# ScalarE's order in the input segments of the mixers: the split of a coming weight panel ahead of the correction copy

## What is computed

```python
def first_block(x, ...):
    for i in range(4):
        h = h + 0.5 * rmsnorm(swiglu(rmsnorm(h, gn[0]), ffn1_w_in[i], ffn1_w_out[i]), gn[1])
        hn = rmsnorm(h, gn[2])
        m = hgrn2_mixer(hn, ...)         # i = 0, 3; diff_attention: i = 1; pool_mixer: i = 2
        h = h + rmsnorm(m, gn[3])
        h = h + 0.5 * rmsnorm(swiglu(rmsnorm(h, gn[4]), ffn2_w_in[i], ffn2_w_out[i]), gn[5])

def second_block(x, ...):                # layer 0: hybrid_mixer, layer 1: recurrent_mixer
    ...

def hgrn2_mixer(x, w_in, gnorm_w, w_out, lb):
    q, f_pre, i_in, g = jnp.split(x @ w_in, ...)         # 1024 x 4096: the input projection
    f = lb + (1.0 - lb) * jax.nn.sigmoid(f_pre); k = 1.0 - f; log_f = jnp.log(f)
    ...                                                  # decayed scores in blocks, state, norm, gate
    return o @ w_out
```

## Time and profile before

| | us |
|---|---|
| median of 3 runs (3299.59 to 3308.34) | 3305.91 |
| the profiled execution, its own time | 3306.95 |
| its span, first to last instruction | 3305.2 |
| TensorE busy (PE) | 3144.2 |
| VectorE busy (DVE) | 2266.2 |
| ScalarE busy (ACT) | 1716.3 |
| mean granted clock of TensorE, share of full speed | 0.975 |
| HBM read, MB | 530.99 |

### The profile page before, as it was taken

The page is one execution under the profiler, slowest core; times in us unless marked ns, Lnnn a source line. Parts: engine busy times, 40 slices in busy tenths (PEclk is TensorE's granted clock), DMA queues, the critical chain, the costliest instruction groups (busy, mean ns, idle before and its releaser), DMA issues.

```text
span 3305.2 us, 44853 instructions
## 1 busy us (share of the span) xinstructions
PE 3144.2 (95%) x18084; PEld 2734.1 (83%) x18084; DVE 2266.2 (69%) x2748; ACT 1716.3 (52%) x2078; POOL 4.3 (0%) x21
## 2 busy tenths in 40 slices
PE   9998999998899999999998899999896999999998
PEld 8886888887688888888887788888774888888887
DVE  7667585867476775675857667585874585866674
ACT  6455554645355554554645555554442464655553
POOL 0000000000000000000000000000000000000000
PEclk9998999999899999999999999999996999999999
DMA  6542355454245454454553245455340255454353
GB/s 228 187 163 102 117 190 191 179 191 140 89 166 191 178 188 171 151 191 166 202 186 134 98 145 191 175 190 184 139 153 13 103 193 191 177 191 163 144 190 128
DMA packets 75358, 534.80 MB, mean 162 GB/s; under 512 B 8480, under 2 KB 8608, under 8 KB 10784
## 3 DMA queue, kind: packets, MB, share of 16 engines
q1 hardware_dynamic: 75168, 532.07, 44.7%
HBM read 530.99 MB, written 1.05 MB: 161 GB/s over the span
## 4 chain that ended last, share of the span: by engine, by line
PE 82%; DVE 8%; ACT 5%; DVEq 3%; issue 1%; DMA 0%; SPq 0%; ACTq 0%
PE pp L1905 33%; PE pp L1906 17%; PE pm L1905 8%; PE pp L2029 4%; PE pm L1906 4%; PE pp L1928 4%; DVE wlo L1675 2%; PE pp L1900 2%; PE pp L1899 2%; PE pp L1901 2%; PE pp L1930 2%; ACT whi L1513 2%; ACT corr L1580 1%; DVE mix L1842 1%; DVEq L395 0%
## 5 line engine op out<-in xcount | busy, mean ns | idle before, releaser
L1905 PE MATMUL pp<-xs,whi 128*128 128x512 f32 x4848 | 1710.1, 397 | 17.5 <-DVE tsum L1755 15.8
L1675 DVE TENSOR_TENSOR wlo<-raw,whi 128x2048 fp32r<-128x2048 f32 x477 | 1090.6, 2289 | 423.8 <-ACT whi L1513 423.0
L1906 PE MATMUL pp<-xs,wlo 128*128 128x256 f32 x4848 | 1357.7, 280 | 0.0
L1905 PEld LDWEIGHTS pp<-xs,whi 128*128 128x128 f32 x4848 | 915.6, 189 | 236.8 <-issue 28.1
L1513 ACT ACTIVATE whi<-raw 128x2048 fp32r<-128x2048 f32 x477 | 910.1, 1911 | 285.7 <-DMA raw<-weights 284.7
L1906 PEld LDWEIGHTS pp<-xs,wlo 128*128 128x128 f32 x4848 | 920.9, 190 | 0.7 <-issue 0.2
L1580 ACT ACTIVATE corr<-pp 128x512 f32<-128x512 f32 x352 | 209.2, 594 | 566.3 <-PE pp L1906 540.9
L1755 DVE TENSOR_TENSOR tsum<-pp,corr 128x512 f32<-128x512 f32 x339 | 233.6, 689 | 297.9 <-ACT corr L1580 297.1
L1905 PE MATMUL pm<-hs,whi 128*128 128x512 f32 x1120 | 393.8, 392 | 0.0
L1906 PE MATMUL pm<-hs,wlo 128*128 128x256 f32 x1120 | 313.2, 280 | 0.0
L1905 PEld LDWEIGHTS pm<-hs,whi 128*128 128x128 f32 x1120 | 210.3, 188 | 43.4
(11 more groups left out here) (330 smaller groups left out, 2989.4 us busy)
## 6 DMA issues: line engine op xcount, KB each, us to landing
raw<-weights SPq DMA_DIRECT2D x503, 1024.0 KB, 4.8
raw<-weights SPq DMA_DIRECT2D x8, 256.0 KB, 7.5
h<-x_by_feature SPq DMA_DIRECT2D x4, 256.0 KB, 6.5
out<-h SPq DMA_DIRECT2D x4, 256.0 KB, 2.5
vec<-vectors SPq DMA_DIRECT2D x1, 264.0 KB, 2.7
lamrow<-diff_lambda SPq DMA_DIRECT2D x1, 128.0 KB, 10.8
skiprow<-ssm_d SPq DMA_DIRECT2D x1, 8.0 KB, 12.5
```

The lines of the kernel that those rows point to most:

```text
L1675: v.tensor_tensor(wlo[:, slot, :], raw[:, slot, :], whi[:, slot, :].bitcast(F32), ALU.subtract).then_inc(sem("weights_lo"), 1)
L1905: mm(bank, whi[:, slot, c:c + P], x_k, start=start, stop=False)
L1906: return mm(bank[:, 0:T], wlo[:, slot, c:c + P], x_k[:, 0:T], start=False, stop=stop)
```

## The change

In `read_out` of ScalarE the split of panel p+4 is made before the wait for the product of panel p, in input segments: in the first one of a mixer from p = 3 on, in HYB's second one for every p. Closing segments keep the old order.

```diff
                 for p in range(seg.wide, seg.panels - closing):
+                    early = not closing and (after_first is None or p >= 3)
+                    if early:
+                        split(seg.g0 + p + AHEAD)
                     act.wait_ge(sem("panel_done"), seg.g0 + p + 1)
                     if seg.wide:
                         act.wait_ge(sem("panel_out"), seg.r0 + p - seg.wide - 1)
                     copy_corr(banks_of(seg, p), (p + seg.first_half) % 2)
                     if after_first is not None and p <= 2:
                         split(seg.g0 + p + AHEAD - 1)
-                    if after_first is None or p >= 2:
+                    if not early and (after_first is None or p >= 2):
                         split(seg.g0 + p + AHEAD)
                     if closing:
                         square_output(s, p - seg.wide)
```

## The result

| | us |
|---|---|
| changed kernel, median of 4 runs (3334.21 to 3341.05) | 3335.51 |
| kernel before, median of 4 runs (3299.59 to 3308.34) | 3305.20 |
| ratio, with its 95% interval | 1.0097 (1.0079 to 1.0115) |
| profiled execution after, its own time (before 3306.95) | 3334.33 |
| its span, with a mean granted clock of 0.972 (before 3305.2, 0.975) | 3332.6 |

The change makes the kernel slower by about 1%. The forecast of 3334 lies 1.5 us from the median. Read by stages it is less exact than that. In the profile after, lines of the kernel behind the edit stand three higher (L1755 is L1758, L1675 is L1678, L1842 is L1845, L1905 is L1908).

The account below looks back on a forecast made before the run. The prediction took the ScalarE-VectorE turn in HGRN, not TensorE, as the bound. HGRN 25.0, DIFF 2.4 and HYB 1.0 sum to 28.4 us on 3306.95, 3335.3; with the median 1.0 lower, 3334 us, range 3326 to 3343.

Parts of the forecast that it names:

- The bound in HGRN: HGRN stages: ScalarE's time between the last step of panel p-1 and what releases VectorE is on the path, once a panel.
- 1.39 a turn, nine times in each stage, 12.5: HGRN: each of nine moved panels a stage takes 1.39 us longer, about 12.5 us a stage, 25.0 us in both.
- 1.80: HGRN, each panel: time lost at the copy because the split holds ScalarE first; also the upper bound for a panel.
- 0.41: Each moved panel: us won at VectorE's wlo, which no longer waits for the split whi.
- What follows the last copy of the stage moves as a block: End of each HGRN stage: everything behind the last copy shifts together, with no further loss.
- The rival of the clock: Three stages: longer TensorE waits bring more lower-clock stretches, up to 16 us, half taken: 8, giving 3342; chance 0.08.
- DIFF +2.4: DIFF: panels 4 and 5 lose 1.39 us each, panels 3 and 6 nothing, panel 7 wins 0.41; sum +2.4 us.
- HYB +1.0: HYB: splits fall mostly into idle time; load landing costs 0.7 us at two copies, 0.41 won once; bounds -8 and +4.
- The sum: Whole kernel: 25.0 + 2.4 + 1.0 = 28.4 us on the profiled 3306.95, giving 3335.3; median predicted 3334 us.
- a gain by idle time: Rival, everywhere: split slips into ScalarE's idle time, wlo never waits, 31 x 0.41 = 12.7 us won, 3293; chance 0.04.
- Slack of two banks: Rival: VectorE's 24.5 us of waits before the addition are slack, so nothing changes, 3306; chance 0.04.
- VectorE slower than reckoned: Rival: 1.80 instead of 1.39 us in all 20 turns, plus HYB's +4, is 40 us, giving 3345; chance 0.04.

Follow-up runs that it names:

- the run that took it away: Changed kernel plus 8 useless TensorE matmuls in the wait before HGRN's tail: HGRN stages 179.4 and 183.4 us, whole 3336.7 us in one run.

## Why the prediction was right, and where it wasn't

- **The bound in HGRN**: ScalarE's time ahead of what releases VectorE, once a panel. Right. HGRN's edit alone gives the loss (3335.48), and an order that lets VectorE's steps go ahead takes 20 us out of each stage.
- **1.39 a turn, nine times in each stage, 12.5**: right, 12.54 and 12.53 in the additions. Both of its parts were tested: 1.80 met alone on top of the other order, 0.41 alone with the split a turn earlier (-7.4 us in all), and half of the split gave 0.54.
- **"What follows the last copy of the stage moves as a block"**: this step failed. TensorE's wait ahead of the tail grew from 1.18 to 4.07 us in the second stage (1.65 to 4.00 in the first), the tail began at 1.2 GHz, and the addition of panel 14 came 2.8 and 3.5 us later than the block. The rival of the clock named the cause: a product that is late. It was put aside with "a product starts two turns before its copy, some 20 us, so even at 1.2 GHz it is ready". That holds for the panels whose copies have 0.0 before them. It fails at panel 14, whose product stands behind the small matmuls of the hook: it started 7.1 us before its copy, and the copy waited for it. The trace of the kernel before has a sign of it, later in the stages than the earlier trace rows reach: this copy already waits 0.78 and 0.67 us for its product. The forecast also took it that nothing waited for slow stretches; in the first stage before, the last group behind a wait of 2.14 us is one, of 1.7 us. The clock cost 6.3 us at panel 14, 4.6 in all by the table, as 1.7 came back by the luck of one slow stretch, and 5.6 by the run that took it away; the rival had 8.
- **DIFF +2.4**: the additions of panels 4, 5 and 6 come 1.8, 3.2 and 2.8 us later against the start of the stage (2.8 forecast for panels 4 and 5), that of panel 7 1.9 and that of panel 8 1.5, where the forecast 0.41 is won. What differs from the forecast appears between the additions of panels 6 and 7, and there unedited kernels differ by -1.1 to +0.3 as well. DIFF's length is 138.7 to 139.8 in six edited profiles and 136.6 to 138.7 in five that have it as before; the sign is right, the size is not settled to better than 1 us.
- **HYB +1.0**: right for what is edited, 1.2 at L1330. Also the mechanism: ScalarE now stands ahead of whi for the load and not ahead of the copy for the product, which answers to the earlier trace rows (groups of ScalarE, 2392 to 2512):

```profile
L1513 ACT ACTIVATE whi<-raw 128x2048 fp32r<-128x2048 f32 x18 | 34.5, 1915 | 43.5 <-DMA raw<-weights 43.5
L1580 ACT ACTIVATE corr<-pp 128x512 f32<-128x512 f32 x18 | 10.5, 584 | 8.4 <-PE pp L1909 8.4
```

  The chain there runs over the load, as the forecast had it for the copy at 2431.65 and the last of the stage:

```profile
2456.28 4.76 DMA raw<-weights
2461.06 1.92 ACT whi L1513
```

  What I left out is that a stage has a scatter of its own: 10 us in the attention loop. A term of 1 us can't be checked by the stage's length, only by a landmark ahead of the loop.
- **The sum** came out at 28.4 forecast and 27.4 in the profiles. HGRN's 4.6 us of clock and HYB's loop of -4.5 stand against each other. The agreement to 1.5 us is partly luck; the part that is not is 25 us in HGRN.
- **The rivals**: a gain by idle time needs copies that wait for TensorE; in HGRN none did. Slack of two banks: the product's wait for the addition grew from 5.1 to 12.7 us, so there was none. VectorE slower than reckoned: in HGRN a turn cost 1.39 and not 1.80, and HYB 1.2 in all (the sum of that rival, 3305.9 + 40, is 3346, not 3345; nothing hangs on it).

## What to carry to other kernels

When two engines hand work back and forth, look at what each does between receiving and giving, not at how busy they are: work for later belongs behind what the other engine waits for, on both sides. Here moving 1.8 us ahead of such a hand-over cost 1% and moving 2.3 us behind one gained 1.2% (1.6% with the other mixers). Of an operation that waits too long for its input, first ask whether the producer can make it a whole turn earlier in the same place (-7.4 us here) before putting it ahead of something urgent. When a stage gets longer waits of TensorE, price the stretch behind each wait at the lower clock too, and look at what stands behind it on TensorE: here a product with no slack stood behind a few small matmuls.

## What was not expected

- The attention loop of HYB, with the same instructions, took 136.1 to 146.1 us in twelve profiles, at a granted clock of 0.87 in the shortest and 0.78 in the two longest. One kernel, profiled twice, differs by 4 us there. What decides in which way the loop falls wasn't tried and stays open. It is 0.3% of the kernel, as large as the spread of its runs.
- Eight useless matmuls in a wait of some 4 us took 2.5 and 3.1 us off the two stages. Whether they would do so in the kernel before, where that wait is 1.18 us in the second stage and the clock behind it 1.00, wasn't tried.
- A matmul on float32 operands that are not rounded copies stands in the trace as two records of 0.22 us each at 256 columns, where after a rounded 256-column one (L1909) the next matmul starts 0.12 us later.
